# Regrouping ScalarE's weight casts and one SiLU in the first mixer, and issuing four state loads earlier

## The reference, cut to what matters

```python
p = h @ w_in                                    # 1024 x 4104
qa, fa, ia, oga, qkv, z, a, bb = split(p)
conv = silu(causal_conv4(qkv))                  # q, k and v of the gated delta heads
g = -exp(a_log) * softplus(a + dt_bias)         # 4 heads per token
beta = sigmoid(bb)
o_b, s_gdn_new = gated_delta_recurrence(l2norm(q), l2norm(k), v, g, beta, s_gdn)
```

## Time and profile before

| What | Value |
|---|---|
| Median of three runs | 1086.85 us (1086.35 to 1086.99) |
| The profiled execution, its own time | 1086.85 us |
| Its span, first to last instruction | 1085.1 us |
| Mean granted PE clock | 0.998 |
| The projection and the gate work beside it on PE | about 225 to 346 us |
| From the first cast that is moved to the end of the SiLU of v | 241.7 to 302.1 us |

### The profile page before, as it was taken

The page is one execution under the profiler, slowest core; times in us unless marked ns, Lnnn a source line. Parts: engine busy times, 40 slices in busy tenths (PEclk is TensorE's granted clock), DMA queues, the critical chain, the costliest instruction groups (busy, mean ns, idle before and its releaser), DMA issues.

```text
span 1085.1 us, 21498 instructions
## 1 busy us (share of the span) xinstructions
PE 1056.2 (97%) x8449; PEld 1033.1 (95%) x8449; DVE 679.8 (63%) x873; ACT 512.0 (47%) x682; POOL 78.0 (7%) x159
## 2 busy tenths in 40 slices
PE   6999999999999998999999999999999999999998
PEld 5999999989899997999999999999999989999997
DVE  5766664468866665776665457666644986666543
ACT  5444443455592443644444346444433554444334
POOL 8100000010000110200000011000000120000001
PEclk9999999999999999999999999999999999999999
DMA  6666655788785420566665558666565437566551
GB/s 198 189 181 174 180 175 188 133 203 170 158 103 174 120 70 28 174 196 174 175 187 178 176 156 248 178 176 179 170 191 178 133 106 209 174 177 187 178 175 40
DMA packets 135062, 177.92 MB, mean 164 GB/s; under 512 B 5806, under 2 KB 120574, under 8 KB 134992
## 3 DMA queue, kind: packets, MB, share of 16 engines
q1 hardware_dynamic: 131616, 165.78, 54.3%
q0 software_dynamic: 3328, 11.38, 3.7%
q10 hardware_dynamic: 64, 0.02, 0.0%
HBM read 171.19 MB, written 6.52 MB: 164 GB/s over the span
## 4 chain that ended last, share of the span: by engine, by line
PE 86%; DVE 7%; ACT 3%; issue 2%; DMA 1%; ACTq 0%; SPq 0%; DVEq 0%
PE ps L1488 25%; PE ps L1489 25%; PE ps L1490 25%; ACT w_hi L513 2%; PE ps L1316 1%; DVE xw_lo L1043 1%; DVE w_lo L1022 1%; PE ps L1323 1%; DVE x L1031 1%; DMA raw<-in_w_in_even 1%; PE ps L1305 1%; DVE PT L983 1%; PE ps L1286 1%; PE ps L1335 1%; PE ps L1603 1%
## 5 line engine op out<-in xcount | busy, mean ns | idle before, releaser
L1022 DVE TENSOR_TENSOR w_lo<-raw,w_hi 128x1024 fp32r<-128x1024 f32 x312 | 381.7, 1226 | 301.6 <-ACT w_hi L513 300.1
L513 ACT CAST w_hi<-raw 128x1024 fp32r<-128x1024 f32 x312 | 325.8, 1049 | 454.2 <-PE ps L1490 431.0
L1488 PE MATMUL ps<-xw_hi,w_hi 128*128 128x264 f32 x1472 | 421.2, 286 | 2.5 <-issue 1.0
L1489 PE MATMUL ps<-xw_lo,w_hi 128*128 128x264 f32 x1472 | 420.2, 285 | 0.0
L1490 PE MATMUL ps<-xw_hi,w_lo 128*128 128x264 f32 x1472 | 419.5, 285 | 0.0
L1488 PEld LDWEIGHTS ps<-xw_hi,w_hi 128*128 128x128 f32 x1472 | 278.5, 189 | 5.2 <-issue 3.8
L1490 PEld LDWEIGHTS ps<-xw_hi,w_lo 128*128 128x128 f32 x1472 | 277.6, 189 | 0.0
L1489 PEld LDWEIGHTS ps<-xw_lo,w_hi 128*128 128x128 f32 x1472 | 277.4, 188 | 0.1
L1490 PE MATMUL ps<-a_hi,w_lo 128*128 (+1 forms) x704 | 200.3, 285 | 0.0
L1488 PE MATMUL ps<-a_hi,w_hi 128*128 (+1 forms) x704 | 200.0, 284 | 0.0
L1489 PE MATMUL ps<-a_lo,w_hi 128*128 (+1 forms) x704 | 200.0, 284 | 0.0
(11 more groups left out here) (340 smaller groups left out, 816.8 us busy)
## 6 DMA issues: line engine op xcount, KB each, us to landing
raw<-in_ffn_w_gate SPq DMA_DIRECT2D x88, 512.0 KB, 3.8
raw<-in_ffn_w_up SPq DMA_DIRECT2D x88, 512.0 KB, 3.8
raw<-in_ffn_w_down SPq DMA_DIRECT2D x88, 512.0 KB, 3.4
raw<-in_w_in_even SPq DMA_DIRECT2D x32, 512.0 KB, 7.7
raw<-in_w_out_even SPq DMA_DIRECT2D x8, 512.0 KB, 4.8
raw<-in_pool_w_in SPq DMA_DIRECT2D x8, 512.0 KB, 3.5
out<-SBUFS POOLq DMA_DIRECT2D x4, 512.0 KB, 4.3
PT<-in_x_prompt SPq DMA_DIRECT2D x2, 512.0 KB
```

The source lines that it names most:

```text
L513: nc.scalar.copy(w_hi[:, w % SPL, :], raw[:, w % RAW, :]).then_inc(hi_done, 1)
L1022: nc.vector.tensor_tensor(w_lo[:, w % SPL, :], raw[:, w % RAW, :], w_hi[:, w % SPL, :].bitcast(F32), ALU.subtract).then_inc(lo_done, 1)
L1488: mm(out, wh, hi, start=first, stop=False)
L1489: mm(out, wh, lo, start=False, stop=False)
```

## The change

On ACT, the casts of slots P+9 (`slots(6, 7)`) and P+10 (`slots(7, 8)`) are moved behind the gate operations, so that the casts of P+9 to P+12 stand together after the logarithm. The SiLU of v, with its wait for `conv` at 2, is moved from behind `slots(18, 22)` to before the wait for `gb_rows_mm`, ahead of the exponential and the copy that signal `bs`. On POOL, the waits for PE's slots P+2, P+6 and P+10 ahead of state loads 0, 1 and 2 are taken out, and load 3 moves from behind the two `CROW` stores to directly behind load 2. No work is added or left out.

```diff
             tap0(4)
-            slots(6, 7)
+
             act.wait_ge(st("gb_u"), 1)
             A.activation(GB[:, 6, :], GB[:, 7, :], ACT.Sigmoid).then_inc(st("beta"), 1)
             link(A.activation(GB[:, 1, :], GB[:, 0, :], ACT.Abs))
             link(A.activation(GB[:, 3, :], GB[:, 1, :], ACT.Exp, scale=-1.0))
-            slots(7, 8)
             A.activation(ab8[:, 2:3], ab8[:, 1:2], ACT.Exp)
             A.activation(GB[:, 4, :], GB[:, 3, :], ACT.Ln, bias=1.0).then_inc(st("gb_ln"), 1)
-            slots(8, 10)
+            slots(6, 10)
             tap0(0)
...
             A.copy(SMALL[:, 0:32], ps[:, 6, 0:32]).then_inc(st("gb_tok"), 1)
+            act.wait_ge(st("conv"), 2)
+            A.activation(C[:, 8:12, :], C[:, 8:12, :], ACT.Silu).then_inc(st("conv_silu"), 1)
 
             act.wait_ge(st("gb_rows_mm"), 1)
             A.activation(SMALL[:, 96:128], ps[:, 7, 0:32], ACT.Exp)
...
             slots(18, 22)
-            act.wait_ge(st("conv"), 2)
-            A.activation(C[:, 8:12, :], C[:, 8:12, :], ACT.Silu).then_inc(st("conv_silu"), 1)
...
-            pool.wait_ge(used, S_PROJ + 3)
             load_state(0)
-            pool.wait_ge(used, S_PROJ + 7)
             load_state(1)
-            pool.wait_ge(used, S_PROJ + 11)
             pool.wait_ge(st("conv_hist_T"), 1)
             load_state(2)
+            load_state(3)
             pool.wait_ge(st("crow"), 1)
             pool.dma_start(conv_p[0, 0], CROW[0:3, :]).then_inc(st("conv_rows_out"), 16)
             pool.dma_start(conv_s[0, :, CONV - 2, :], CROW[3:11, :]).then_inc(st("conv_rows_out"), 16)
-            load_state(3)
```

## The result

The change makes the kernel slower: 1095.18 us in the median of four runs (1093.80 to 1096.49), against 1086.92 us for the kernel before measured beside it (1086.35 to 1088.46). The ratio is 1.0075, with a 95% interval of 1.0059 to 1.0090. The loss is 8.3 us, where 5.0 were forecast, and the time lies 0.6 us above the range. The profiled execution took 1092.95 us (span 1091.2), the shortest of all that were timed; the others had a lower mean clock of PE (0.994 to 0.995, this one 0.996). The profile therefore shows 6.1 us of the loss. The remaining 2.2 us go with the lower clock of the other executions, which have no profile.

What follows compares the result with a forecast made beforehand. PE, busy 97% of the span, was taken as the bound. The casts' and SiLU's lateness share one chain through DVE and ACT, state loads cost 0: 1086.85 + 5.0 = 1091.85, taken as 1091.8 us; range 1090.2 to 1094.6.

Steps and rivals of the forecast that it cites:

- P+8, 2.38 us late: On PE, P+8 waits for DVE's `evac(2)`, delayed by the regrouped casts, and starts at 251.64 instead of 249.26.
- That idle time is used up: DVE's 1.78 us idle for `tap0(0)` absorbs part of its 5.08 us lateness, leaving P+12 3.30 us late.
- If that transfer is no longer what ACT waits for: Condition on P+16's transfer, for which ACT's cast waited 2.54 us; then `tap0(8)` on ACT is 1.38 us late.
- The late transfer: Rival: P+16's weight transfer, sent later, takes 9.0 us and lengthens the chain by 1.9 us: 1093.7 us; chance 0.15.
- the 7.2 us that it had: P+16's transfer, sent at 261.4, may land until ACT's cast at 268.6 at no cost.
- Part 3: Early state loads on POOL: cost 0, P+8's transfer with 2.3 us to spare, ACT's transfer waits covered by DVE's lateness.
- the 0.35 us of the prediction: By `evac(5)`, DVE wins 0.35 us it had waited for a cast, so it is 2.95 us late.
- Part 2: SiLU of v before `bs`: PE's sum of squares starts 5.0 us late; SiLU's wait alone 3.6 us.
- The clock: Rival: PE's clock falls once after a new stall, costing 1.70 us: 1093.5 us; chance 0.08.
- its own stalls of 2.4 and 2.2 us: Forecast new PE stalls: 2.4 us from P+8's wait for `evac(2)`, 2.2 us before the sum of squares.
- the bound of 0.9: Most the early state loads could gain: PE's 0.94 us idle before P+12 and P+16, taken as 0.9 us.

Runs made afterwards that it cites:

- e6: Changed kernel, but the transfers of P+14 and P+15 read block 4 of the input weights instead of block 3 (wrong weights): 1094.23 us, ratio 1.0061.
- e4: Changed kernel, but DVE does `evac(3)` earlier, directly behind `tap(4, 1)`: 1096.08 us, ratio 1.0084.
- e7: Changed kernel with both `evac(3)` moved earlier on DVE and block 4 read for P+14 and P+15 (wrong weights): 1092.59 us, ratio 1.0052.
- e2: Kernel before with only the SiLU of v moved ahead of `bs`: 1092.68 us, ratio 1.0051.
- e1: Kernel before with only the four casts regrouped: 1092.72 us, ratio 1.0052.
- e5: Changed kernel with idle-filling float32 matmuls on PE, five before P+8's wait and five before the sum of squares: 1093.65 us.
- e8: Kernel before with state loads issued early, `evac(4)` moved up on DVE and filling matmuls ahead of the first mixer's root: 1083.78 us, ratio 0.9970.
- e3: Kernel before with only POOL's state loads issued early: 1085.27 us, ratio 0.9986.
- e10: Changed kernel with filling matmuls in the gaps at 222.8 and 423.1 us and before P+8, P+10, P+12 and the sum of squares: 1091.38 us.
- e9: Kernel before with five filling matmuls in each of two gaps, at 222.8 and 423.1 us: 1085.82 us, ratio 0.9995.

## Why the prediction was wrong, point by point

- **P+8, 2.38 us late: right** (2.49). ACT's regrouped casts hold up `w_lo` of P+9, `evac(2)` behind it, and PE.
- **"That idle time is used up": wrong.** This is the first step that failed, and the one in the walk itself. The prediction let `tap0(0)` wait only for the cast of P+12 ahead of it. Its own wait is for `p_ready` at 4, which is `evac(3)`, and that stands behind the late low part on the same DVE queue. So DVE idled the same 1.78 us as before, and P+12 was 5.18 us late in place of 3.30. The 1.9 us stayed in the chain: v's last tap was 3.27 us late in place of 1.38, and the sum of squares 7.06 in place of 5.0.
- **"If that transfer is no longer what ACT waits for": true of P+16, and it missed the two ahead of it.** The late transfer was a rival with a chance of 0.15, priced for P+16 alone, and the case against it was that a state load had shared the queues. P+16's did take 6.7 us then, in place of 9.0 and inside the 7.2 us that it had. The slow ones are P+14 and P+15, 9.2 and 10.4 us, and they are slow by what they read (e6). Part 3 held that ACT's waits for such transfers are covered by DVE's lateness. They are not: SP sends a transfer when a low part of DVE has ended, so it sent these two 5.2 us later than before, and ACT's casts of them waited as long as before. In the changed kernel this cost nothing beyond the first obstacle, for `evac(5)` was 4.83 us late, which is 5.18 less the 0.35 us of the prediction. This obstacle and the previous one stand one behind the other: taking away the first alone gained nothing (e4), the second alone nothing certain (e6), and both together gave back 2.0 us at the sum of squares, down to the forecast 5.0 (e7). P+15's transfer holds `evac(5)` where the late queue of DVE held it.
- **Part 2: right.** The SiLU's wait ended when the last tap of v did, and `bs` came 287.51 - 284.84 = 2.67 us after the SiLU began, for which 1.09 + 1.57 = 2.66 was the sum. Alone it makes the sum of squares 3.38 us late, where its least was worked out as 3.6. ACT has one instruction less (681 for 682), the table load that was to go. Casts and SiLU share one chain and don't add up, as said. The table load of 1.28 us began 0.02 us after the SiLU's end, so there was no drain beside it. The Trainium skill's 2.66 us for a switch (ScalarE: Activation LUTs, section "What ACT_TABLE_LOAD costs") don't agree with that row.
- **Part 3: right that it costs nothing**; alone it gives 0.8 us, inside the bound of 0.9. P+8's transfer was cast from 235.46 us on, and ACT idled 2.75 us between that cast and its copy of the history at 239.26; 2.3 us to spare were forecast. The Trainium skill's rule that all issuing engines share the 16 DMA engines (DMA: Bandwidth & Descriptors, section "Issuing engines are not separate DMA queues") agrees with P+8's transfer, which took 10.7 us beside the two states and 7.8 before; there was room for both kinds.
- **The clock: left out of the sum, wrongly.** It had a chance of 0.08 and 1.7 us for one fall, and this is the term that cost the most of the miss. The price of a fall is right where PE is the bound: 1.72 us behind the SiLU's stall in e2. How often was not. The prediction read 2.59 us of idle time at 222.8 and called its own stalls of 2.4 and 2.2 us nearly as long. 2.59 us is the length of that stretch, in which PE was busy for 0.39; the idle time before P+2 was 2.20 us. The forecast stalls were as long as the one after which the clock fell in the kernel before, and those measured, 2.29 and 2.40 us, were longer. Filled, the changed kernel loses 3.8 us of its time, of which the kernel without the change has a part as well; 2.0 to 2.7 us are left for the change. In the profiled execution the fall at 252.7 cost nothing at P+12: P+8 and P+9 ran slower into a time in which PE would have waited for DVE anyway. Where the falls lay in the runs that have no profile is not known, so the split between places stays open.

The sum, then: waits of 7.1 us at the sum of squares, 5.0 of them as forecast and 2.0 for the two obstacles. With the clock kept up on both sides they come to 5.6 to 6.3 us, and the clock has the rest of the 8.3. Of the 3.3 us by which the loss was missed, that is 0.6 to 1.3 us for the waits and 2.0 to 2.7 us for the clock. The waits come out smaller here than in the first profile, as the filled kernel before waits 0.9 us longer at P+16 than the unfilled one.

## What to carry to other kernels

When an instruction is late and the next engine's idle time is to absorb it, look up every wait of the instruction that ends this idle time: if one of them is behind the late instruction itself, the idle time moves along and absorbs nothing. An experiment that removes one obstacle and gains nothing has not cleared it, for another may stand right behind; remove both before dropping either. A wait for a transfer is not covered by lateness ahead of it, if the same lateness delays the sending. In a kernel bound by TensorE, compare each new idle stretch with those of the profile at hand after which the clock fell, idle time with idle time.

## What the runs showed of the hardware that was not expected

- **The time of a transfer depended on the columns it read.** Slots of 512 KB read 1 KB pieces at a row pitch of 16416 bytes. Blocks 4 to 6 took 5.2 us in the median; block 3 took 9.2 and 10.4 us; with block 4 read at the same moment it was 4.7. Block 7 in the kernel before took 8.9 us, in the median of its two transfers. Why these blocks are slow was not tested further.

```profile
raw<-in_w_in_even SPq DMA_DIRECT2D x2, 512.0 KB, 8.9
```

- **The same idle stretch is followed by a fall of the clock in some executions and not in others.** Behind the 2.20 us before P+2 the clock fell in all nine profiles where PE idled there, and in none of the five where that time was filled. Behind the stall of 2.24 to 2.29 us before P+8 it fell in three of five (the changed kernel, e1 and e4; not in e6 and e7). Behind the 1.91 us at 422 to 434 us it fell in five of ten (e2, e5, e6, e7 and e8; not in the kernel before, the changed one, e1, e3 and e4). And one fall of 3.41 us cost 1.72 us in one place and 1.15 in another (e2), or nothing (at 252.7 in the changed kernel).
- **Useless matmuls made the kernel faster.** e10 does 27 matmuls more than the changed kernel and is 3.8 us faster, at a mean clock of 0.998 to 1.000 in place of 0.994 to 0.996. Ten such matmuls in two gaps of the kernel before gave nothing clear by themselves (e9); in its profile, transfers set the pace behind the first gap.
